# Order of the mixer's steps: attention sums and halves, weight halves, query rotation, filter copies

## The reference, cut to what matters

```python
h = modulate(rmsnorm_2(x, norm1_g[i]), sh1, sc1)
q, k, v, hv, hx1, hx2, gna, ghy = jnp.split(h @ w_in[i], IN_SPLITS, axis=-1)
y_na = neighbourhood_attention(q, k, v, k_c, v_c, rpb)   # rotate q, k; scores; softmax; times v
y_hy = hyena_mixer(hv, hx1, hx2, ...)   # 3-tap conv; filters; twice: gate * ifft(fft(z) * K)
m = jax.nn.sigmoid(gna) * (y_na @ w_na_o) + jax.nn.sigmoid(ghy) * (y_hy @ w_hy_o)
x = x + g1 * (m @ w_out)
```

## Time and profile before

| | |
|---|---|
| median of 3 runs | 1033.98 us (1031.92 to 1034.25) |
| the profiled execution | 1030.56 us |
| its span, first to last instruction | 1028.7 us |
| mean granted TensorE clock | 0.990 |
| busy: PE / DVE / ACT / POOL | 995.1 / 790.2 / 557.3 / 22.2 us |

### The profile page before, as it was taken

One profiled execution on the slowest core, in us unless ns is written; L12 is line 12 of the kernel. 1 busy time (PEld: TensorE's weight loads), 2 busy tenths in 40 slices (PEclk: granted clock), 3 DMA queues, 4 the chain that ended last, 5 costly groups with the idle time before them and its releaser, 6 DMA issues.

```text
span 1028.7 us, 19808 instructions
## 1 busy us (share of the span) xinstructions
PE 995.1 (97%) x7928; PEld 963.6 (94%) x7928; DVE 790.2 (77%) x1409; ACT 557.3 (54%) x931; POOL 22.2 (2%) x28
## 2 busy tenths in 40 slices
PE   9999999999899999999999897899989999999997
PEld 5999999999899999999999897788979999999996
DVE  5888889966999789988887667679786787676553
ACT  5654444345777565555545366575534565545442
POOL 4000000000000000000000000000001100000000
PEclk9999999999999999999999999899999999999998
DMA  8666667983433268876787125343324465555441
GB/s 291 221 206 217 224 221 239 317 287 124 145 123 124 83 238 298 306 230 213 240 283 245 45 64 160 111 124 123 103 83 146 164 224 167 197 171 185 159 148 41
DMA packets 53573, 187.49 MB, mean 182 GB/s; under 512 B 6120, under 2 KB 7689, under 8 KB 53034
## 3 DMA queue, kind: packets, MB, share of 16 engines
q1 hardware_dynamic: 53306, 185.64, 54.1%
q10 hardware_dynamic: 176, 0.59, 0.1%
HBM read 185.16 MB, written 1.05 MB: 181 GB/s over the span
## 4 chain that ended last, share of the span: by engine, by line
PE 75%; DVE 16%; ACT 5%; issue 3%; DMA 0%; DVEq 0%; POOL 0%; ACTq 0%; POOLq 0%
PE psum L441 74%; DVE memr L991 6%; DVE memr L1013 3%; ACT memr L1680 1%; DVE mem L1194 1%; DVE memr L1197 1%; ACT mem L1691 1%; ACT memr L1691 1%; DVE mem L1188 1%; ACT mem L2006 1%; PE psum L456 1%; DMA mem<-in_w_up 0%; ACT mem L1822 0%; DVE mem L1590 0%; DVE mem L1154 0%
## 5 line engine op out<-in xcount | busy, mean ns | idle before, releaser
L441 PE MATMUL psum<-memr 128*128 128x256 f32 (+5 forms) x7652 | 958.7, 288 | 21.0 <-DVE memr L1013 14.9
L441 PEld LDWEIGHTS psum<-memr 128*128 128x128 f32 (+1 forms) x7652 | 931.5, 189 | 41.3 <-issue 22.2
L991 DVE TENSOR_TENSOR memr<-mem,memr 128x1024 fp32r<-128x1024 f32 (+1 forms) x290 | 337.4, 1199 | 66.0 <-ACT memr L1680 65.8
L1680 ACT ACTIVATE memr<-mem 128x1024 fp32r<-128x1024 f32 (+2 forms) x296 | 290.7, 1025 | 20.1 <-PE psum L441 9.0
L1691 ACT ACTIVATE memr<-mem 128x256 fp32r<-128x256 f32 (+4 forms) x171 | 81.4, 484 | 280.7 <-DVE mem L1123 104.0
L1013 DVE TENSOR_TENSOR memr<-mem,memr 128x256 fp32r<-128x256 f32 (+2 forms) x129 | 61.5, 484 | 10.9 <-ACT memr L1691 9.9
L1108 DVE TENSOR_TENSOR mem<-psum,mem 128x256 f32<-128x256 f32 (+1 forms) x66 | 28.0, 424 | 44.6 <-PE psum L441 44.6
L1001 DVE CUSTOM_DVE_ANT_0 mem<-mem 128x1024 f32<-128x1024 f32 x48 | 58.6, 1221 | 0.6
L1688 ACT ACTIVATE mem<-mem 128x256 f32<-128x256 f32 (+1 forms) x56 | 22.8, 413 | 64.8 <-DVE mem L1647 31.9
L1013 DVE TENSOR_TENSOR memr<-psum,memr 128x256 fp32r<-128x256 f32 (+2 forms) x72 | 32.3, 461 | 16.6 <-ACT memr L1691 15.7
L1691 ACT ACTIVATE memr<-psum 128x256 fp32r<-128x256 f32 (+3 forms) x80 | 29.6, 400 | 15.1 <-PE psum L441 11.1
(11 more groups left out here) (131 smaller groups left out, 384.4 us busy)
## 6 DMA issues: line engine op xcount, KB each, us to landing
mem<-in_w_gate SPq DMA_DIRECT2D x66, 512.0 KB, 4.1
mem<-in_w_up SPq DMA_DIRECT2D x66, 512.0 KB, 4.5
mem<-in_w_ada SPq DMA_DIRECT2D x48, 512.0 KB, 4.6
mem<-in_w_down SPq DMA_DIRECT2D x48, 448.0 KB, 4.4
mem<-in_w_in SPq DMA_DIRECT2D x40, 512.0 KB, 4.4
mem<-in_w_down SPq DMA_DIRECT2D x24, 512.0 KB, 4.7
mem<-in_sb_qkv SPq DMA_DIRECT2D x24, 512.0 KB, 4.6
mem<-in_sb_o SPq DMA_DIRECT2D x8, 512.0 KB, 3.4
```

The source lines that it names most:

```text
L441: return pe.matmul(out, a, b, start=start, stop=stop)
L991: dve.tensor_tensor(r(ol, n), raw(e), rf(oh, n), ALU.subtract).then_inc(w_lo, 1)
L1680: act.activation(r(oh, n), raw(e), ACT.Copy).then_inc(w_hi, 1)
```

## The change

The work is the same, and its order on PE, DVE, ACT and SP changes.

- The split of tile 0 (q0) stands ahead of the first key rotation (DVE) and of its high copy (ACT).
- `softmax_sums(p)` and `softmax_scale(p)` stand directly behind `softmax(p)` for p = 1 to 3; `weights_high/low(p)` for p = 1, 2 ahead of the rotation of the next query; the splits (`used`) move behind them and have other numbers.
- Tile g6 stands between h7 and h8 in place of behind h9, and is evicted by a plain copy (`EARLY` 7); `early_gates` moves behind h_step(10).
- PE has h5's gemm ahead of filter_tile(0), g6 ahead of spectrum(0), h10 ahead of spectrum(1).
- On DVE h_conv(5) stands ahead of filter_tile(0), and the eight `final_norm` products ahead of matrix_low(1); on ACT the high copies of a filter tile come in two parts with h_step, h_rows and splits between.
- SP's waits for softmax and the transfers of bias, W3, matrices and decay stand up to three tiles earlier in the order of the weight tiles.

```diff
-MIX_TILES = ("q0 q1 h0 h1 g0 q2 g1 h2 g2 q3 g3 h3 h4 g4 g5 h5 h6 h7 h8 h9 g6 h10 h11 g7 g8 ...
+MIX_TILES = ("q0 q1 h0 h1 g0 q2 g1 h2 g2 q3 g3 h3 h4 g4 g5 h5 h6 h7 g6 h8 h9 h10 h11 g7 g8 ...
-EARLY = 6
+EARLY = 7
@@ PE @@
         na_attend(3)
+        h_mm(5)
         ...
         filter_tile(0)
-        h_mm(5)
         h_mm(6)
+        h_rows(5)
         h_mm(7)
-        h_rows(5)
+        g_mm(6)
         pe.wait_ge(table_lo, 2)
         spectrum(0)
         filter_tile(1)
         ...
         h_mm(9)
-        g_mm(6)
+        h_mm(10)
         spectrum(1)
-        h_mm(10)
         h_mm(11)
@@ DVE @@
         v_rows_low(3)
+        low_halves(W_MIX + 1)
         k_step(0)
-        low_halves(W_MIX + 1)
         ...
         softmax(1)
+        softmax_sums(1)
         u_low(0)
         h_conv(1)
-        softmax_sums(1)
-        used(4)
         v_rows_low(7)
-        used(5)
+        weights_low(1)
         q_step(2)
         q_turned(2)
-        used(6)
-        weights_low(1)
+        used(5)
         na_low(1)
         softmax(2)
+        softmax_sums(2)
         u_low(1)
+        used(6)
+        h_conv(2)
+        weights_low(2)
         used(7)
-        h_conv(2)
-        softmax_sums(2)
-        used(9)
         q_step(3)
         q_turned(3)
-        used(10)
-        weights_low(2)
-        used(11)
+        used(9)
         na_low(2)
         softmax(3)
+        softmax_sums(3)
         u_low(2)
         h_conv(3)
-        softmax_sums(3)
-        used(12)
+        used(10)
         h_conv(4)
-        used(13)
+        weights_low(3)
         u_low(3)
-        used(14)
-        weights_low(3)
         dve.wait_ge(table_hi, 1)
         minus(r(W3S, 2048, 64, 128), f(W3R, 2048, 0, 64), rf(W3S, 2048, 0, 64)).then_inc(table_lo, 1)
-        used(15)
+        used(13)
         na_low(3)
+        used(14)
         matrix_low(0)
+        h_conv(5)
+        used(15)
         filter_tile(0)
-        h_conv(5)
         h_conv(6)
+        h_conv(7)
         used(18)
-        h_conv(7)
         filter_tile(1)
         h_conv(8)
         h_conv(9)
-        used(21)
+        used(20)
+        ... (the eight final_norm products)
+        h_conv(10)
+        used(22)
         matrix_low(1)
-        h_conv(10)
         h_conv(11)
         used(23)
         transform(0)
         used(26)
-        ... (the eight final_norm products)
@@ ACT, from head pair 3 on @@
         softmax(3)
+        softmax_scale(3)
         h_rows(2)
         h_step(3)
-        softmax_scale(3)
-        used(12)
+        used(10)
         h_step(4)
+        weights_high(3)
         h_rows(3)
-        used(13)
-        gate(4)
-        used(14)
-        weights_high(3)
         act.wait_ge(w3_in, 16)
         copy(r(W3S, 2048, 0, 64), f(W3R, 2048, 0, 64)).then_inc(table_hi, 1)
+        gate(4)
+        used(13)
         gate(5)
         h_rows(4)
-        used(15)
         na_high(3)
+        used(14)
         matrix_high(0)
-        early_gates()
-        filter_tile(0)
         h_step(5)
+        used(15)
+        filter_high(0, 0)
         h_step(6)
+        h_rows(5)
+        used(16)
+        filter_high(0, 1)
+        h_step(7)
+        used(17)
+        gate(6)
         used(18)
-        h_rows(5)
-        h_step(7)
         spectrum(0)
+        filter_high(1, 0)
         h_rows(6)
-        filter_tile(1)
         h_step(8)
         h_rows(7)
+        filter_high(1, 1)
         h_step(9)
-        gate(6)
-        used(21)
+        used(20)
+        h_step(10)
+        early_gates()
+        used(22)
         spectrum(1)
         matrix_high(1)
-        h_step(10)
         h_step(11)
@@ SP @@
-        for p, end in enumerate((8, 13, 17)):
+        for p, end in enumerate((8, 13, 16)):
         ...
-        raws(W_MIX + 22)
+        raws(W_MIX + 20)
         ...
-        raws(W_MIX + 24)
+        raws(W_MIX + 21)
```

More of the change, by code:

```diff
@@ L94, in neighbour_bias @@
     return np.ascontiguousarray(np.concatenate([x.transpose(0, 2, 1, 3) for x in halves], axis=1).reshape(8, 128, 384))
-MIX_TILES = ("q0 q1 h0 h1 g0 q2 g1 h2 g2 q3 g3 h3 h4 g4 g5 h5 h6 h7 h8 h9 g6 h10 h11 g7 g8 g9 g10 g11 g12 g13 g14 "
+MIX_TILES = ("q0 q1 h0 h1 g0 q2 g1 h2 g2 q3 g3 h3 h4 g4 g5 h5 h6 h7 g6 h8 h9 h10 h11 g7 g8 g9 g10 g11 g12 g13 g14 "
              "g15").split()
 KV_ORDER = (0, 1, 2, 4, 3, 5, 6, 7)
-EARLY = 6
+EARLY = 7
 W_POOL = 0
@@ L1581, in vector @@
         h_conv(9)
-        used(21)
+        used(20)
+        for i in range(KT):
+            dve.scalar_tensor_tensor(hx(i, NMETA, T1), hx(i, NMETA, T1), vec("final_norm", i), f(SROOT, T1),
+                                     ALU.mult, ALU.mult)
+        h_conv(10)
+        used(22)
         matrix_low(1)
-        h_conv(10)
         h_conv(11)
@@ L1588, in vector @@
         used(26)
-        for i in range(KT):
-            dve.scalar_tensor_tensor(hx(i, NMETA, T1), hx(i, NMETA, T1), vec("final_norm", i), f(SROOT, T1),
-                                     ALU.mult, ALU.mult)
         dve.wait_ge(x1_cp, 4)
@@ L2050, in scalar @@
         k_step(0)
+        high_halves(W_MIX + 1)
         k_turned(0)
-        high_halves(W_MIX + 1)
         k_step(1)
@@ L2079, in scalar @@
         softmax(1)
+        softmax_scale(1)
         h_rows(0)
         h_step(1)
-        softmax_scale(1)
-        used(4)
         gate(0)
         v_rows_high(7)
-        used(5)
+        weights_high(1)
         q_step(2)
         q_turned(2)
-        used(6)
-        weights_high(1)
         gate(1)
+        used(5)
         na_high(1)
         softmax(2)
+        softmax_scale(2)
         h_rows(1)
+        used(6)
+        h_step(2)
+        gate(2)
+        weights_high(2)
         used(7)
[L2096 to L2099, removed]
         q_step(3)
         q_turned(3)
-        used(10)
-        weights_high(2)
         gate(3)
-        used(11)
+        used(9)
         na_high(2)
         softmax(3)
+        softmax_scale(3)
         h_rows(2)
         h_step(3)
-        softmax_scale(3)
-        used(12)
+        used(10)
         h_step(4)
+        weights_high(3)
         h_rows(3)
-        used(13)
-        gate(4)
-        used(14)
-        weights_high(3)
         act.wait_ge(w3_in, 16)
         copy(r(W3S, 2048, 0, 64), f(W3R, 2048, 0, 64)).then_inc(table_hi, 1)
+        gate(4)
+        used(13)
         gate(5)
         h_rows(4)
-        used(15)
         na_high(3)
+        used(14)
         def matrix_high(n):
@@ L2130, in matrix_high, with filter_high @@
             copy(r(MATH, 1024), f(MATR, 1024)).then_inc(table_hi, 1)
[L2132 to L2139, removed]
+        def filter_high(n, t):
+            for i in range(2):
+                act.wait_ge(fl_dve, 13 * n + (4, 10)[t] + i)
+                if n and not t:
+                    act.wait_ge(sp_mm, 4)
+                src = (PSUM_, SPARE[1])[i] + 512 * t
+                copy(r(PM + 2048 * i + 512 * t, 512), f(src, 512)).then_inc(pm_hi, 1)
         def spectrum(n):
```

## The result

| | before | changed |
|---|---|---|
| median (range), 4 runs each | 1033.23 us (1031.92 to 1034.25) | 1019.01 us (1017.45 to 1019.51) |
| the profiled execution, its span | 1030.56, 1028.7 us | 1019.51, 1017.7 us |
| mean granted clock | 0.990 | 0.991 |
| busy PE / DVE / ACT | 995.1 / 790.2 / 557.3 us | 993.5 / 790.1 / 558.1 us |

The account below looks back on a forecast made before the run. TensorE, 97% busy, bounds the kernel; 25.2 us of gaps and clock minus 13.05 new gives 12.2, absolute starts give 14.1, the middle 13.2 is taken. With 3.4 us carried to the median: 1020.8 us, range 1014.5 to 1025.5.

Parts of the forecast that it names:

- before spectrum(0): PE gap of 2.6 us before spectrum(0), released by the filter tile's last subtraction on DVE, in place of h_rows(5)'s 2.52.
- the one that spoke against the change: Head pair 3: scale copies ahead of h_step(3) delay h_conv(3) to 668.0, a 4.55 us PE gap before h_rows(3).
- The clock: Lower clock charged once among the new gaps, 1.6 us more behind the gap before h_rows(3).
- rival (b): Gaps before spectrum(0) and transform(0) lose the clock too, 1.7 us each: 1022.5 to 1024.2 us; chance 0.22.
- The step from the profiled execution to the median: Median 1033.98 lies 3.4 us above the profiled 1030.56; that difference is carried over, giving 1020.8.
- the reading by absolute starts: transform(1) comes at 745.55 in place of 757.98; with 1.7 us of clock behind it the gain is 14.1 us.
- that by differences of idle rows: 25.2 us to be had minus 13.05 us of new gaps and clock: gain of 12.2 us.
- What the clock cost before: 36 matmuls of attend and scores took 6.27 and 5.93 us instead of 4.3: 2.0 and 1.6 to 1.7 lost.
- The cause before transform(0): ACT's early_gates and spectrum(1) ahead of the matrix copy delay matrix_low(1): a 2.05 us PE gap before transform(0).
- Rival (a): No gap before h_rows(3), as ACT or DVE reach softmax(3) early enough: 6.1 us less, 1014.7 us; chance 0.20.
- rival (c): VectorE is the bound, so gaps only change places: 3 us or less left, 1031 to 1034 us; chance 0.05.
- (d): Slower: SyncE holds back h10 and h11, stalling ACT at used(17), then spectrum(0) and PE: 1038 us; chance 0.03.

Follow-up runs that it names:

- the two kernels above: Changed kernel with softmax_sums(3)/softmax_scale(3) back behind h_conv(3)/h_step(3), 1015.36 us; changed kernel with PE's h_rows(3) moved behind na_turn(3), 1013.09 us.

## Why the prediction was right

By its own steps, forecast and measured:

| step | forecast | changed kernel |
|---|---|---|
| before q0 | 0.15 | 0.16 |
| before na_attend(1), (2) | 0, 0 | 0, 0 |
| before g3 | 0.4 | 0.25 |
| before scores(3) | 1.25 | 0.93 |
| before h_rows(3) | 4.55 | 4.53 |
| before h5 | 0.45 | 0.70 |
| before spectrum(0) | 2.6 | 2.63 |
| before transform(0) | 2.05 | 2.01 |
| before back transform, transform(1) | 0, 0 | 0, 0 |
| sum | 11.45 | 11.21 |
| clock lost, places | 1 | 3 |

The reading of the gaps held at every place to within 0.35 us, and the one that spoke against the change was right too: the scale copies in front of h_conv(3), shown by the two kernels above that remove that gap or more than half of it from either side.

Four things in it were off. **The clock**: I charged one loss of 1.6 us, behind h_rows(3). The profiled execution has three in the mixer, as rival (b) had them: g4's 24 matmuls took 4.25 us for 3.05 (1.2), the 32 behind spectrum(0)'s gap 9.12, where the execution with gates and products moved took 7.52 (1.6), and there is one behind transform(0)'s gap. It has a fourth at 265 us, in a part that the change leaves alone. In this execution, then, rival (b)'s mechanism came true, and not mine.

**The step from the profiled execution to the median**: that 1020.8 lies so near to 1019.01 was luck, two errors that cancel. From before's profiled execution (1030.56) the forecast gain of 13.2 leads to 1017.4. The changed kernel's took 1019.51, 2.1 more, with two clock losses that I didn't charge: the profiled executions are only 11.05 us apart, inside rival (b)'s 9.8 to 11.5. But I had added the 3.4 us by which before's profiled execution lay under its median, and the changed kernel's lies 0.5 above its own. Those 3.4 us are no fixed amount that a kernel carries along. Of 27 later executions of the kernel before, the seven with a mean clock of 0.990 or 0.991 took 1029.98 to 1030.48 us, and the eighteen with 0.985 or 0.986 took 1031.02 to 1034.72; the profiled one, at 0.990, was of the quick kind. So the medians' 14.2 doesn't decide between the reading by absolute starts (14.1) and that by differences of idle rows (12.2).

**What the clock cost before**: I took 4.3 us for the 36 matmuls of attend and scores at full clock. The kernel with the attention of pairs 1 and 2 back has them at 1.00 in 4.58 us, from 661.44 to the next group at 666.02. Against that the two losses were 1.7 and 1.35 us in place of 2.0 and 1.6 to 1.7, and what could be had was some 0.6 us less than 25.2.

**The cause before transform(0)**: I named ACT's early_gates alone, with final_norm lying "under ACT's work". It was two chains of equal length, and the kernel with the gates moved shows that mine alone was not enough. The size was right, by half of the cause. Besides, I gave the filter copies in two parts a share in the end of h_rows(5)'s gap, by letting h_step(6) and (7) through. With the copies whole there is no such gap. That h_conv(5) ahead of the filter tile ends it is my reading; no kernel tests it alone. The two parts are worth 1 us of the gap before transform(0).

Rival (a) is out for the changed kernel, rival (c) too, and (d): ACT goes through the place in question, from 696.00 to 699.50, without a pause. Rival (b)'s losses were there, its time of 1022.5 to 1024.2 was not. What it quoted of the Trainium skill ("TensorE: Matmul & The Clock Gate", Part 1) is said there of the start of a kernel, where the number of slow matmuls is run-variable. The traces show the like behind gaps in mid-kernel: the same gap lost the clock in 9 executions and kept it in 5; the last section has the rows.

The page "ScalarE: Activation LUTs" of the Trainium skill has a drain behind the table's load. In the changed kernel the load at its new place is again followed 0.02 us behind its end by the next activation, and nothing of the 1.4 us shows:

```profile
716.00 1.28 ACT L2042 ACT_TABLE_LOAD   x1
717.30 1.80 ACT L2042 ACTIVATE mem<-mem 128x1024 f32<-128x1024 f32 x2
```

## What to carry to other kernels

In a hand-written order, ask of each group of copies that the busy engine waits for which instructions stand in front of it on the copying engine and whether they need to; here rotation or splits alone cost nothing that the times could tell, and together with late scale copies they made gaps of 5.0 us, so count against the room there is. Moving a group forward pushes the ones behind it, and the place to look is the next point at which the busy engine comes by with no slack (here h_rows(3), 0.15 us). When a gap is ended by an instruction that two engines feed, both chains are to be followed to their ends before one of them is shortened.

## What the runs showed of the hardware

The lower clock doesn't follow from the length of a gap alone. Up to some 580 us all these kernels do the same in the same order, and each has a gap of 3.28 or 3.29 us at 261 us. In 9 of the 14 profiles the clock fell behind it, in 5 (the kernel before among them) it stayed. The stretches from 265 to 270 us, before and changed:

```profile
265.00:270.00 5.00, 5.00 (x39) 4.75 (x39) 4.96 (x11) 3.75 (x9) 0.00 (x0) 1.00 0.34 133
```

```profile
265.00:270.00 5.00, 5.00 (x30) 4.74 (x30) 4.97 (x12) 3.71 (x10) 0.00 (x0) 0.69 0.23 93
```

In the mixer the 14 profiles have 32 gaps of PE between 1.8 and 2.8 us. Behind 20 of them the clock was at the lower level in the 3 us that followed, for part or all of it, behind 12 it was at 1.00 throughout; length doesn't part them (1.86, 1.89 and 1.98 us are among the lowered; 2.52, 2.63 and 2.64 occur among both). It was lowered behind each of the twelve gaps of 3 us or more, and behind none of those from 0.86 to 1.6 us. The execution with final_norm back kept 1.00 behind its 2.64, 2.00 and 1.58; that with the rotation first lost it behind 1.86, 2.41, 2.64 and 1.99. Where it is lost, it costs 1.2 to 2.6 us by the rows above: 4.25 for 3.05, 9.12 for 7.52, 7.24 for 4.65. So such a gap has its length as a sure price, and the clock as a chance; the runs of one kernel differ by up to 5 us. With the rotation first three took 1020.10 to 1020.30 at a mean clock of 0.989 and one 1015.06 at 0.994, which agrees with that; which gaps kept the clock in the quick one isn't shown, as it has no profile.
